# SBUF addresses of matmul operands: moving the high and low weight parts and the operands to chosen distances modulo 256 bytes

## The reference, cut to what matters

```python
z = h @ w_in[l]                                        # 1024 -> 7424, and so for every projection
x = x + gate_f * ((silu(u_gate) * u_val) @ w_down[l])  # feed-forward layers
y = (silu(xe @ w1[e]) * (xe @ w3[e])) @ w2[e]          # one expert
```

## Time and profile before

| | |
|---|---|
| runs | 2057.45, 2056.92, 2056.99 us; median 2056.99 us |
| profiled execution | span 2055.1 us from its first to its last instruction, 32745 instructions |
| TensorE matmul busy | 2009.1 us, 98% of the span, 13665 matmuls |
| weight loads busy | 1791.2 us, 87% |
| VectorE, ScalarE busy | 1703.8 us, 83%; 1256.9 us, 61% |
| mean granted TensorE clock | 0.990 |
| DMA | 589.16 MB, mean 287 GB/s |

### The profile page before, as it was taken

How to read it: one execution, slowest core, us unless ns; L and a number is a source line. 1 busy time by engine, 2 the same in 40 slices (tenths; PEclk the granted TensorE clock), 3 DMA queues, 4 the chain that set the end, 5 groups by cost and what they waited for, 6 DMA issues and landing times.

```text
span 2055.1 us, 32745 instructions
## 1 busy us (share of the span) xinstructions
PE 2009.1 (98%) x13665; PEld 1791.2 (87%) x13665; DVE 1703.8 (83%) x1874; ACT 1256.9 (61%) x1269; POOL 39.5 (2%) x77
## 2 busy tenths in 40 slices
PE   7999999999899999999999999999999999999997
PEld 6899999999879899999878888888888888888886
DVE  6787988988786768887479898898888988898987
ACT  3468745654434454443367777777777777777775
POOL 3010000000000000000000000000000000000000
PEclk8999999999999999999999999999999999999999
DMA  9874776768643459999259999999999999999994
GB/s 310 290 249 137 244 248 198 261 224 292 207 161 123 138 170 332 316 316 323 84 204 369 369 342 373 344 372 355 356 358 352 365 352 367 357 348 372 361 370 157
DMA packets 337576, 589.16 MB, mean 287 GB/s; under 512 B 10517, under 2 KB 150315, under 8 KB 337424
## 3 DMA queue, kind: packets, MB, share of 16 engines
q1 hardware_dynamic: 333776, 580.70, 80.7%
q0 software_dynamic: 3008, 5.78, 1.1%
q10 hardware_dynamic: 640, 0.52, 0.1%
HBM read 585.89 MB, written 1.07 MB: 286 GB/s over the span
## 4 chain that ended last, share of the span: by engine, by line
PE 89%; DVE 5%; ACT 2%; issue 2%; DMA 1%; SPq 0%; DVEq 0%; ACTq 0%
PE bk L657 15%; PE bk L659 15%; PE bk L658 15%; PE bk L651 11%; PE bk L653 11%; PE bk L652 11%; DVE wlo L1957 1%; DVE macc L1982 1%; PE bk L1202 1%; ACT whi L1339 1%; DMA raw<-in_w_mod 1%; PE bk L1251 1%; PE bk L713 1%; PE bk L1114 1%; PE bk L715 1%
## 5 line engine op out<-in xcount | busy, mean ns | idle before, releaser
L1957 DVE TENSOR_TENSOR wlo<-raw,whi 128x2048 fp32r<-128x2048 f32 x477 | 1080.9, 2268 | 223.1 <-ACT whi L1339 222.2
L1339 ACT CAST whi<-raw 128x2048 fp32r<-128x2048 f32 x477 | 903.2, 1894 | 389.5 <-PE bk L659 259.0
L651 PE MATMUL bk<-HH,whi 128*128 128x256 f32 x1480 | 425.1, 287 | 0.7 <-DVE KC L2233 0.4
L652 PE MATMUL bk<-HL,whi 128*128 128x256 f32 x1480 | 417.5, 282 | 0.0
L653 PE MATMUL bk<-HH,wlo 128*128 128x256 f32 x1480 | 417.2, 282 | 0.0
L657 PE MATMUL bk<-whi,xh 128*128 128x512 f32 x896 | 354.6, 396 | 0.0
L659 PE MATMUL bk<-wlo,xh 128*128 128x512 f32 x896 | 349.4, 390 | 0.0
L658 PE MATMUL bk<-whi,xl 128*128 128x512 f32 x896 | 348.7, 389 | 0.0
L651 PEld LDWEIGHTS bk<-HH,whi 128*128 128x128 f32 x1480 | 282.4, 191 | 6.4 <-issue 3.8
L652 PEld LDWEIGHTS bk<-HL,whi 128*128 128x128 f32 x1480 | 282.5, 191 | 1.1 <-issue 0.7
L653 PEld LDWEIGHTS bk<-HH,wlo 128*128 128x128 f32 x1480 | 282.4, 191 | 0.0
(11 more groups left out here) (378 smaller groups left out, 2471.5 us busy)
## 6 DMA issues: line engine op xcount, KB each, us to landing
raw<-in_moe_w SPq DMA_DIRECT2D x334, 1024.0 KB, 6.1
raw<-in_ada_w SPq DMA_DIRECT2D x56, 1024.0 KB, 5.5
raw<-in_ff_w SPq DMA_DIRECT2D x40, 1024.0 KB, 5.8
raw<-in_w_in SPq DMA_DIRECT2D x29, 1024.0 KB, 5.4
raw<-in_w_mod SPq DMA_DIRECT2D x24, 1024.0 KB, 5.8
raw<-in_w_up SPq DMA_DIRECT2D x22, 1024.0 KB, 5.2
raw<-in_attn_w_qkv SPq DMA_DIRECT2D x12, 1024.0 KB, 5.5
raw<-in_w_branch SPq DMA_DIRECT2D x8, 1024.0 KB, 4.9
```

What stands on the lines that cost most here:

```text
L651: pe.matmul(o, sh, mh, start=start, stop=False, skip_group_check=True)
L652: pe.matmul(o, sh, ml, start=False, stop=False, skip_group_check=True)
L1339: act.copy(whi[k][:, :n], raw[q.slot[i]][:, :n]).then_inc(q.hi_done.mark(g), 1)
L1957: dve.tensor_tensor(wlo[k][:, :n], raw[q.slot[i]][:, :n], whi[k][:, :n].bitcast(F), ALU.subtract).then_inc(q.taken.mark(i), 1)
```

## The change

`sb` takes a place, and puts the buffer at the next address that has this value modulo 256. The `whi` buffers go to 128, the `wlo` buffers to 64 with 64 bytes of room behind their 2048 values. All pairs that move in 256-column products go to 32. XH, XL, TT and TTL go to 128. The experts' slabs use `wlo` from its 16th value on, so at 64 + 64 = 128; all other slabs use it from its start. GS moves behind YH and YL, which thereby come to 128, as PB and PTT do.

So the distance of a moving operand from its stationary one changes as follows: 32 - 128 = 160 modulo 256 for HH or HL against `whi`, and 32 - 64 = 224 against `wlo` (both 0 before, 32 in the second feed-forward layer and the Fourier projection); for `natural` 96 and 32 (0 before); 0 for w1 and w3 as before; 0 for w2 (before 0 - 96 = 160); 0 for the scatter (before 160). Number, order and sizes of the instructions, and all waits, stay.

```diff
-        def sb(name, shape, dt=F):
+        def sb(name, shape, dt=F, place=None):
+            if place is not None:
+                at[0] += (place - at[0]) % 256
             t = nc.alloc_sbuf_tensor_at(name, shape, dt, offset=at[0])
...
-        whi = [sb(f"whi{i}", [128, 2048], R) for i in range(NP)]
-        wlo = [sb(f"wlo{i}", [128, 2048], R) for i in range(NP)]
+        whi = [sb(f"whi{i}", [128, 2048], R, 128) for i in range(NP)]
+        wlo = [sb(f"wlo{i}", [128, 2064], R, 64) for i in range(NP)]
...
-        HH, HL = sb("HH", [128, 8, S], R), sb("HL", [128, 8, S], R)
+        HH, HL = sb("HH", [128, 8, S], R, 32), sb("HL", [128, 8, S], R, 32)
...
-        OH, OL = sb("OH", [128, 16, S], R), sb("OL", [128, 16, S], R)
+        OH, OL = sb("OH", [128, 16, S], R, 32), sb("OL", [128, 16, S], R, 32)
...
-        HH4, HL4 = sb("HH4", [128, 8, S], R), sb("HL4", [128, 8, S], R)
-        FH4, FL4 = sb("FH4", [128, 28, S], R), sb("FL4", [128, 28, S], R)
+        HH4, HL4 = sb("HH4", [128, 8, S], R, 32), sb("HL4", [128, 8, S], R, 32)
+        FH4, FL4 = sb("FH4", [128, 28, S], R, 32), sb("FL4", [128, 28, S], R, 32)
...
-        XH = [sb(f"xh{i}", [128, 8, 256], R) for i in range(2)]
-        XL = [sb(f"xl{i}", [128, 8, 256], R) for i in range(2)]
+        XH = [sb(f"xh{i}", [128, 8, 256], R, 128) for i in range(2)]
+        XL = [sb(f"xl{i}", [128, 8, 256], R, 128) for i in range(2)]
         PB = sb("pb", [128, 2, 256], R)
         PTT = [sb(f"ptt{i}", [128, 2, 256], R) for i in range(2)]
+        TT = [sb(f"tth{i}", [128, 4, 128], R, 128) for i in range(2)]
+        TTL = [sb(f"ttl{i}", [128, 4, 128], R, 128) for i in range(2)]
+        YH, YL = sb("YH", [128, 1024], R), sb("YL", [128, 1024], R)
         GS = [sb(f"gsl{i}", [128, 2]) for i in range(3)]
-        TT = [sb(f"tth{i}", [128, 4, 128], R) for i in range(2)]
-        TTL = [sb(f"ttl{i}", [128, 4, 128], R) for i in range(2)]
-        YH, YL = sb("YH", [128, 1024], R), sb("YL", [128, 1024], R)
...
+        lies = {"w1": 16, "w3": 16, "w2": 16}
+        def halves_at(q, g):
+            i = q.gi[g]
+            e, n, k = lies.get(q.plan[i][1][0], 0), q.plan[i][3] * q.plan[i][4], g % NP
+            return whi[k][:, :n], wlo[k][:, e:e + n]
```

More of the change, by code:

```diff
@@ L266, in build @@
         at[0] = base
-        HHc, HLc = sb("HHc", [128, 8, S], R), sb("HLc", [128, 8, S], R)
-        HH2, HL2 = sb("HH2", [128, 8, S], R), sb("HL2", [128, 8, S], R)
+        HHc, HLc = sb("HHc", [128, 8, S], R, 32), sb("HLc", [128, 8, S], R, 32)
+        HH2, HL2 = sb("HH2", [128, 8, S], R, 32), sb("HL2", [128, 8, S], R, 32)
         mark = at[0]
-        FH, FL = sb("FH", [128, 22, S], R), sb("FL", [128, 22, S], R)
+        FH, FL = sb("FH", [128, 22, S], R, 32), sb("FL", [128, 22, S], R, 32)
         UC = [sb(f"uc{i}", [128, 2, S]) for i in range(3)]
@@ L295, in build @@
         FN = sb("FN", [128, 2, 8, 256])
-        HH5, HL5 = sb("HH5", [128, 8, S], R), sb("HL5", [128, 8, S], R)
+        HH5, HL5 = sb("HH5", [128, 8, S], R, 32), sb("HL5", [128, 8, S], R, 32)
         at[0] = mark
@@ L642, in slab @@
             assert q.plan[i][1] == tag, (q.plan[i][1], tag)
-            k, nk, w = q.pg % NP, q.plan[i][3], q.plan[i][4]
+            nk, both = q.plan[i][3], halves_at(q, q.pg)
             pe.wait_ge(*(yield from q.taken.of(i)))
             q.pg += 1
-            return [v[:, :nk * w].rearrange("p (k n) -> p k n", k=nk) for v in (whi[k], wlo[k])] + [nk]
+            return [v.rearrange("p (k n) -> p k n", k=nk) for v in both] + [nk]
         def three(o, stationary, moving, start, stop):
@@ L1334, in act_hi @@
             i = q.gi[g]
-            n, k = q.plan[i][3] * q.plan[i][4], g % NP
+            n = q.plan[i][3] * q.plan[i][4]
             if g >= NP:
@@ L1338, in act_hi @@
             act.wait_ge(q.raw_in[q.slot[i]], 16 * q.use[i])
-            act.copy(whi[k][:, :n], raw[q.slot[i]][:, :n]).then_inc(q.hi_done.mark(g), 1)
+            act.copy(halves_at(q, g)[0], raw[q.slot[i]][:, :n]).then_inc(q.hi_done.mark(g), 1)
         sq_user = {}
@@ L1951, in dve_lo @@
                 return
-            i, k = q.gi[g], g % NP
-            n = q.plan[i][3] * q.plan[i][4]
+            i = q.gi[g]
+            n, (high, low) = q.plan[i][3] * q.plan[i][4], halves_at(q, g)
             if q is st:
@@ L1956, in dve_lo @@
             dve.wait_ge(*(yield from q.hi_done.of(g)))
-            dve.tensor_tensor(wlo[k][:, :n], raw[q.slot[i]][:, :n], whi[k][:, :n].bitcast(F), ALU.subtract).then_inc(q.taken.mark(i), 1)
+            dve.tensor_tensor(low, raw[q.slot[i]][:, :n], high.bitcast(F), ALU.subtract).then_inc(q.taken.mark(i), 1)
         vm, acc_told = [0], {}
```

## The result

The kernel after takes 2041.51 us (median of 4 runs, 2040.59 to 2044.15) against 2056.95 for the kernel before (4 runs, 2055.01 to 2057.45): ratio 0.993, 95% interval 0.9917 to 0.9942. It is faster by 15.4 us. The forecast was 2020.0, so 37 us: the sign and the range held, the size did not. The profiled execution's span went from 2055.1 to 2040.5 us, and that 14.6 us is what the traces can be asked about.

What follows compares the result with a forecast made beforehand. TensorE was taken as the bound, busy 98% of the span and 89% of the chain of waits. 2055.1 - 27.4 (256-column products) - 9.7 (w2) = 2018.0 us of span, plus 1.9 for the runs, say 2020; range 1995 to 2050.

Steps and rivals of the forecast that it cites:

- w2: Experts' w2 products, distance 160 to 0: steps from 233.9 to 226.7 ns, 9.7 us less; bounds 0 and 9.7.
- TT's place: Lower bound of the w2 saving: 0 if the price hangs on TT's position and not on the distance.
- The DMA rival: Experts: 1% less time asks DMA for 361 GB/s; if not to be had, 9.7 us stays unsaved, 2029.6; chance 0.10.
- The price of the 256-column step: 256-column products at 160 and 224: a step of 115 ns, range 113 to 124.8, 27.4 us less in all.
- I take 115, between 113 and 116.7: Choice of 115 ns for the 256-column step, over the 118.2 that the two nearest rows alone would say.
- the order of the two widths: Distance 0 is low at 512 columns, high at 256, so a distance poor at 512 may be good at 256.
- So both terms count in full: VectorE stays under TensorE in the first feed-forward layer and the experts, so 27.4 and 9.7 us reach the end.
- Slower: Rival: at 160 moving stream and weight load meet more often; 256-column mean 124.8 ns, 30.9 us more, 2088; chance 0.10.
- Nothing changes: Rival: step differences come from the stage and not from addresses, time stays 2057; chance 0.07.
- No help at 256 columns: Rival: all 256-column steps take the scatter's 119 ns; with w2, 9.3 us less, 2048; chance 0.15.
- Below 113: Rival: the weight load stops mattering, 256-column steps under 113 ns, time under 2006, 1978 by the skill's estimate; chance 0.06.
- The warning at the end of the prediction: Prediction is wrong above all if two distances differing for high and low part don't act like a mean of single ones.

Runs made afterwards that it cites:

- experiment 1: Kernel before with only GS moved, so w2 and the scatter come to distance 0: 2047.34 us against 2056.58, ratio 0.9955.
- experiment 4: Scan against the kernel after: each slab's weights at an offset of its own, distances in steps of 32 and pairs; one execution, 113.3 to 120.0 ns per 256-column step.
- Experiment 2: Kernel after with GS back ahead of TT, so w2 and scatter stay at 160 and only the 256-column part changes: 2050.0 us, ratio 0.9971.
- Experiment 7: Kernel after with 256-column operands at 64 and low parts at 0, so high at 192, low at 64: 2019.8 us against 2055.98, ratio 0.9822.
- experiment 3: Kernel after with wlo at 128 like whi, so all three loads of a 256-column product lie at 160: 2045.1 us, ratio 0.9942.
- experiment 6: Experiment 4's kernel with other offsets: pairs with 192, finer steps; one execution, high 192 with low 64 at 113.3 ns, (160, 224) at 117.8.
- Experiment 8: Second feed-forward up products: every other slab at 192 and 192, thirteen other pairs between; one execution, the 192 slabs at 113.3 to 113.5 or 117.8 ns.

## Why the prediction was right in sign and wrong in size

**w2, right.** 1344 x 7.2 = 9.7 us: 9.9 in the trace after, 9.9 in the trace of experiment 1 (9.2 by its runs), 0.1 where w2 kept 160. Of its bounds, TT's place is out by experiment 4. The DMA rival is out, at 362 GB/s.

**The price of the 256-column step, wrong.** The step that failed is "I take 115, between 113 and 116.7". The prediction's own nearest rows gave 118.2: the scatter at 160, and 32 as the mirror of 224. With 118.2 the sum would have been 4728 x 1.8 = 8.5 us, less 2208 x 1.5 = 3.3, and 9.7 more for w2, together 14.9, and the forecast 2057.0 - 14.9 = 2042.1; 2041.51 was measured. What set it aside was an argument from the order of the two widths: 0 is good at 512 columns and bad at 256, so 160, bad at 512, might be good at 256. The scan gives no such order: 96 is the same high price as 0 at 256 columns and among the high ones at 512, 192 is the best at 256 and no better than 32 at 512. (The mean of 0.115 us read from the four steps of the earlier trace rows came of rounding; unrounded it is 116.5 ns.) Experiment 2 measures the term by itself: some 6 us, not 27.4. The working also priced the 528 `natural` products with the rest, though the change puts them at 96 and 32; in the attention they went from 119.8 to 118.4.

That 118.2 came out so near is partly luck. The steps measured about 117.6 from 119.9, and 117.8 from 117.2 where 116.7 had been read from one good stretch, so 9.6 us were offered, of which 4.7 had arrived when the experts began; by the runs of experiment 2 it was some 6. A step priced too high and a path taken as clear made up for each other.

**"So both terms count in full", wrong for the 256-column part.** VectorE did stay under in the first feed-forward layer's up half, which kept its whole 2.5 us. But the working looked at that one stretch. The down half's 1.4 us were not to be had, as the chain there ran through VectorE and ScalarE in the kernel before already; the output projection's 0.8 turned into waiting, the attention kept 1.4 of 2.4, and a stretch of lower clock took 1.2 us more in this execution. Experiment 7 has the same in large: 34.3 us offered, 26.3 arrived.

**Rivals.** "Slower" by 160 meeting the load more often: no unbroken run of steps at (160, 224) was above about 118, and that stream and load meet is not shown by any trace, which has the steps' lengths alone. "Nothing changes" is refuted by the experiments, where moving buffers alone takes 6 to 36 us off. "No help at 256 columns" (119, 2048) was nearer in kind than the forecast, but 117.8 is not 119, and its total is 6.5 us off. "Below 113" did not come, not even at 192: the lowest in any run is 113.3. The Trainium skill's page "TensorE: Matmul & The Clock Gate" (Back-to-back issue gap) gives N / 2.4 + 2.5 ns for a matmul by itself, an estimate of 109.2 for 256 columns, and says that in a stream with weight loads both set the spacing; the best distance found stays 4.1 ns above 109.2. The 1978 that the prediction has by it is a span; as a time of the runs it would be 1980. The Trainium skill's same page (Part 2, Step-by-step: what each phase is for) has two independent read ports, so that weight loads take no bandwidth from the stream; by that the address should not matter, and 113.3 to 120 ns by nothing but the address disagrees.

**The warning at the end of the prediction** came true: two distances for the high and low part don't act like a mean of the single ones (experiments 3, 4 and 6).

**What stays open.** Why 192 and 64 (and 0 at 512 columns) are good, and why a slab keeps the rhythm that it settled in: the runs show which step each distance had, not what inside the chip makes it, and with one slab for most pairs not every rhythm that a pair allows. Of the gain that did not arrive, the stretches named explain the greater part; the boundaries between slabs in the mixer and the attention were not followed one by one.

## What to carry to other kernels

Where TensorE is the bound, the distance between the moving and the stationary operand, modulo 256 bytes, is a parameter to scan on the chip for each width and each order of the products; here it was worth 36 us in 2056 with no instruction changed, and at 512 columns 4 bytes off the good value cost more than the change of distance had won. Try a distance in more than one slab, as one slab shows one of its rhythms. Price an unseen case by its nearest rows, and let an argument from analogy widen the range, not move the value. And read the chain of waits stage by stage before a faster step is counted in full: where the stage's own products are not in it, the step is worth nothing.

## What the runs showed of the hardware that was not expected

- The same 256-column product runs at 113.3, 115.6, 116.7, 117.4, 117.8, 118.7 or 120.0 ns from start to start at a granted clock of 1.00, and nearly every slab keeps one of these to its end once it has settled.
- One pair of addresses allows several: (160, 224) 115.6 and 117.8, (160, 160) 117.4, 118.7 and 120.0, (192, 192) and (64, 64) 113.3 and 117.8. Experiment 8 shows that at (192, 192) how the slab is entered decides.
- The good distance depends on the width: 192 and 64 at 256 columns (113.3 in some slabs), 0 at 512 columns (227, with 236.7 four bytes on).
- The order counts within a round: high 192 with low 64 had 113.3 to 114.2 in every slab of the feed-forward layers' up products, high 64 with low 192 119.0 in each of two slabs.
